# A recurrent layer's input projection: weights and input split into high and low parts, three products in place of one

## The reference, cut to what matters

```python
hn = rmsnorm(h, pre_mix_g[i])
proj = hn @ rwkv_w_in[j]                       # 1024 x 2816, float32
prev = jnp.pad(proj, ((0, 0), (1, 0), (0, 0)))[:, :-1]
xs = proj + (prev - proj) * mu                 # shift by one token
r, k, v, wl, al, gl = jnp.split(xs, offs, axis=-1)
w = -jax.nn.softplus(-(w0 + jnp.tanh(wl) @ w2)) - 0.5
a = jax.nn.sigmoid(a0 + al @ a2)
g = jax.nn.sigmoid(gl) @ g2
kk = kk * lax.rsqrt(jnp.maximum(jnp.sum(kk * kk, axis=-1, keepdims=True), 1e-24))
```

## Time and profile before

| What | Value |
| --- | --- |
| median of three runs | 764.7 us (764.57 to 766.06) |
| the profiled execution | 763.77 us, span in the trace 762.0 us |
| TensorE busy | 720.8 us, 95% of the span |
| VectorE, ScalarE, GpSimd busy | 444.2, 393.3, 106.8 us |
| recurrent strips in the span | 363.9 to 456.6 us |
| chunk phase begins | 463.56 us |

### The profile page before, as it was taken

One profiled execution on the slowest core, in us unless ns is written; L12 is line 12 of the kernel. 1 busy time (PEld: TensorE's weight loads), 2 busy tenths in 40 slices (PEclk: granted clock), 3 DMA queues, 4 the chain that ended last, 5 costly groups with the idle time before them and its releaser, 6 DMA issues.

```text
span 762.0 us, 15191 instructions
## 1 busy us (share of the span) xinstructions
PE 720.8 (95%) x6549; PEld 619.1 (81%) x6549; DVE 444.2 (58%) x645; ACT 393.3 (52%) x655; POOL 106.8 (14%) x163
## 2 busy tenths in 40 slices
PE   4999998999999999999999998987799999999997
PEld 3789975678888888888888878986678888888885
DVE  3778777646865675532243548642657757656523
ACT  5744776547655555532465536533258554556311
POOL 8121066700000000000300055700000000000000
PEclk9999989999999999999999999999999999999999
DMA  8846710007665565653844331000028565655511
GB/s 301 320 143 198 272 56 2 2 0 256 215 201 186 183 204 171 211 172 113 270 136 156 111 111 58 4 6 4 3 84 276 180 206 168 206 180 185 203 55 56
DMA packets 78277, 111.71 MB, mean 147 GB/s; under 512 B 2124, under 2 KB 64738, under 8 KB 78210
## 3 DMA queue, kind: packets, MB, share of 16 engines
q1 hardware_dynamic: 77090, 107.67, 42.3%
q0 software_dynamic: 976, 3.04, 1.3%
q10 hardware_dynamic: 144, 0.04, 0.0%
HBM read 109.68 MB, written 1.05 MB: 145 GB/s over the span
## 4 chain that ended last, share of the span: by engine, by line
PE 87%; DVE 5%; ACT 4%; issue 2%; DMA 1%; POOL 0%; DVEq 0%; SPq 0%; ACTq 0%; POOLq 0%
PE ps L1060 20%; PE ps L746 10%; PE ps L747 10%; PE ps L748 10%; PE ps L1063 10%; PE ps L1048 8%; PE ps L1225 5%; PE ps L1235 4%; PE ps L780 2%; PE ps L866 2%; PE ps L889 2%; DVE w_lo L1889 2%; PE ps L915 1%; DMA hn<-mem 1%; ACT w_hi L1416 1%
## 5 line engine op out<-in xcount | busy, mean ns | idle before, releaser
L1889 DVE TENSOR_TENSOR w_lo<-w_raw,w_hi 128x2048 fp32r<-128x2048 f32 (+2 forms) x90 | 202.2, 2260 | 84.4 <-ACT w_hi L1416 84.3
L1060 PE MATMUL ps<-x_hi_lo,w_hi 128*128 128x512 f32 x640 | 201.2, 396 | 0.0
L1416 ACT ACTIVATE w_hi<-w_raw 128x2048 fp32r<-128x2048 f32 (+2 forms) x90 | 168.1, 1887 | 39.4 <-PE ps L748 38.2
L1063 PEld LDWEIGHTS ps<-x_hi_lo,w_lo 128*128 128x128 f32 x640 | 120.2, 188 | 28.4
L1063 PE MATMUL ps<-x_hi_lo,w_lo 128*128 128x256 f32 x640 | 125.7, 278 | 0.0
L1060 PEld LDWEIGHTS ps<-x_hi_lo,w_hi 128*128 128x128 f32 x640 | 97.4, 189 | 0.0
L746 PE MATMUL ps<-w_hi,x_hi_lo 128*128 128x512 f32 (+3 forms) x208 | 74.0, 356 | 5.2 <-DVE x_hi_lo L2117 3.4
L748 PE MATMUL ps<-w_hi,x_hi_lo 128*128 128x512 f32 (+3 forms) x208 | 72.0, 346 | 0.0
L747 PE MATMUL ps<-w_lo,x_hi_lo 128*128 128x512 f32 (+3 forms) x208 | 71.9, 346 | 0.0
L746 PE MATMUL ps<-w_hi,hidden_hi 128*128 128x512 f32 x176 | 68.6, 390 | 0.0
L747 PE MATMUL ps<-w_lo,hidden_hi 128*128 128x512 f32 x176 | 68.5, 389 | 0.0
(11 more groups left out here) (367 smaller groups left out, 984.7 us busy)
## 6 DMA issues: line engine op xcount, KB each, us to landing
w_raw<-w_ffn_in SPq DMA_DIRECT2D x44, 1024.0 KB, 5.1
w_raw<-w_ffn_out SPq DMA_DIRECT2D x22, 1024.0 KB, 4.9
w_raw<-rwkv_w_in SPq DMA_DIRECT2D x11, 1024.0 KB, 5.1
w_raw<-w_out SPq DMA_DIRECT2D x8, 1024.0 KB, 5.0
w_raw<-nsa_w_in SPq DMA_DIRECT2D x6, 1024.0 KB, 14.5
w_raw<-w_mem_kv SPq DMA_DIRECT2D x2, 1024.0 KB, 9.4
w_raw<-nsa_cmp_k_w SPq DMA_DIRECT2D x2, 1024.0 KB, 5.7
w_raw<-nsa_cmp_v_w SPq DMA_DIRECT2D x2, 1024.0 KB, 5.4
```

The lines of the kernel that those rows point to most:

```text
L1060: pe.matmul(psum[:, bank + j, :], kt_of(w_hi, i, k)[:, cols[j]], xx[:, k, :, :].rearrange("p c n -> p (c n)"), start=k == 0, stop=False)
L1063: ins = pe.matmul(psum[:, bank + j, 0:SEQ], kt_of(w_lo, i, k)[:, cols[j]], xh[:, k, :], start=False, stop=k == KD - 1)
L1416: act.activation(w_hi[:, i % SPL, 0:size(i)], raw[:, i % RAW, 0:size(i)], ACT.Copy).then_inc(hi_done, 1)
L1889: dve.tensor_tensor(w_lo[:, i % RAW, 0:size(i)], raw[:, i % RAW, 0:size(i)], w_hi[:, i % SPL, 0:size(i)], ALU.subtract).then_inc(lo_done, 1)
```

## The change

`whole` and all that hung on it is removed. Pieces of the recurrent projection go through the same copy on ScalarE and subtraction on VectorE as all others; join 1 writes `x_hi_lo` in place of `x_rwkv`, as the other joins do; and both kinds of strip form each product by `three`. The positions of the `split_to` calls are not touched, but those that did nothing now split. The semaphore counts follow. Cut to its core:

```diff
         def tile_base(m, t):
-            return (0, 8, 12)[m] + (2 if m == 1 else 4) * t
+            return 4 * (TT * m + t)
@@ tok_strip
-                if whole(i):
-                    pe.wait_ge(landed[i % RAW], land_value[i])
-                else:
-                    pe.wait_ge(lo_done, split_no(i) + 1)
+                pe.wait_ge(lo_done, i + 1)
                 for k in range(KD):
-                    if whole(i):
-                        if part == 0 and k % 2 == 0:
-                            pe.wait_ge((j_hi, j_lo)[k // 2 % 2], tile_base(m, t) + k // 4 + 1)
-                        ins = pe.matmul(psum[:, turn_bank(m, t) + part, 0:FC], xf[:, k, tile(t)], raw_kt(i, k),
-                                        start=k == 0, stop=k == KD - 1)
-                        continue
@@ feature_strip
-                pe.wait_ge(landed[i % RAW], land_value[i])
+                pe.wait_ge(lo_done, i + 1)
                 for j in range(2):
                     c = slice(P * j, P * j + P)
                     for k in range(KD):
-                        ins = pe.matmul(psum[:, bank, j * SEQ:(j + 1) * SEQ], raw_kt(i, k)[:, c], xf[:, k, :],
-                                        start=k == 0, stop=k == KD - 1)
+                        ins = three(psum[:, bank, j * SEQ:(j + 1) * SEQ], kt_of(w_hi, i, k)[:, c], kt_of(w_lo, i, k)[:, c],
+                                    xh[:, k, :], xl[:, k, :], start=k == 0, stop=k == KD - 1)
@@ tile_hi (tile_lo: the same for the other four slices)
-                    if m == 1:
-                        if k // 2 % 2 == 0:
-                            ins = act.activation(xf[:, k, tile(t)], quarter(m, t, k), ACT.Copy, scale=colA[:, col:col + 1])
-                            if k % 2:
-                                ins.then_inc(j_hi, 1)
-                        continue
```

More of the change, by code:

```diff
@@ L170, in trunk @@
         xh, xl = xx[:, :, 0, :], xx[:, :, 1, :]
-        xf = at(o_x, "x_rwkv", [P, KD, SEQ])
         o_hn = base[0]
@@ L1023, in full_gemm @@
                     if t == 0:
-                        pe.wait_ge(lo_done, split_no(i0 + j) + 1)
+                        pe.wait_ge(lo_done, i0 + j + 1)
                         if j < n_ready:
@@ L1885, in split_to @@
                 for i in range(split[0], min(n, NPIECES)):
-                    if whole(i):
-                        continue
-                    dve.wait_ge(hi_done, split_no(i) + 1)
+                    dve.wait_ge(hi_done, i + 1)
                     dve.tensor_tensor(w_lo[:, i % RAW, 0:size(i)], raw[:, i % RAW, 0:size(i)], w_hi[:, i % SPL, 0:size(i)],
@@ L2106, in tile_lo @@
                     col = NORM_COL[m + 2] + k
[L2107 to L2114, removed]
                     if k % 2 == 0:
```

## The result

The changed kernel took 770.16 us, the median of 10 runs (767.84 to 775.23); the kernel before, on the same chip, 765.57 us (10 runs, 764.52 to 766.83). The ratio is 1.0054, its 95% interval 1.0039 to 1.0070: slower by half a per cent. The forecast was 769.0 us against a median of 764.7, so +4.3 us; measured +4.6.

A forecast was written before the change was run, and what follows sets the result against it. TensorE owned 87% of the chain, but ScalarE's and VectorE's written order was to decide: +4.9 - 0.6 = +4.3 us at the chunk phase turns 763.77 into 768.1; with 0.93 to the median, 769.0 us (767.8 to 770.6).

The forecast's parts named there:

- (g): Split 10 delays the receptances' last shift: first row maximum 6.5 us later, TensorE waits about 4 us inside strip 9.
- (a): Behind the first feed-forward layer: pieces 0 and 1 are split in ScalarE's 17.06 us of idle, at no cost.
- (b): At the join: eight high parts on ScalarE, eight low on VectorE; two token strips save 2.3 us and pay 0.65.
- (c): Join's end: splits 2, 3, 4 precede the `strip_tok` copies; TensorE waits 1.3 us, leaving 0.35 of 1.65 us gained.
- (d): Strip 2 saves 1.15 us: second lora group starts at 387.35 instead of 388.83, but `vT` ends at 406.5 as before.
- (e): Splits 7, 8 on ScalarE and low parts 8, 9 on VectorE delay the `kk_squares`: end at 420.95, before 418.53.
- (f): ScalarE's logarithm comes at 421.0, strip 6's copy ends at 429.5; TensorE stands still 6.2 us ahead of strip 8.
- (h): VectorE catches up where it formerly waited: second probabilities' turn 4.9 us later, chunk products at 467.9 instead of 463.56.
- Spare time enough: Rival: splits land in idle moments of ScalarE and VectorE, 9.6 us saved, 755 us; chance 0.08.
- Slow steps: Rival: strip products' three steps are no faster than now, 0.144 us each, giving 772 us; chance 0.03.
- Cancel: Rival: low parts 8 and 9 finish before the head sums, logarithm at 418.5 as before, 763.5 to 766 us; chance 0.13.
- The clock: Rival: TensorE's holes halve its clock; strips 8, 9 cost 0 to 0.4 us, strip 10 1.2 to 2.4; 770 to 773; chance 0.2.

The follow-up runs named there:

- the filled hole: The changed kernel with 14 full-precision matmuls of constants put into TensorE's wait ahead of strip 8; 772.8 us, ratio 1.0093 to the kernel before.
- reordered: The changed kernel with all splits kept, their copies on ScalarE and subtractions on VectorE moved to later places; 761.48 and 760.65 us, ratios 0.9920 and 0.9881.
- the join's order alone: The changed kernel with only the join moved: ScalarE writes the first tile's token-shift strip ahead of splits 3 and 4, third copy still behind; 770.8 us, ratio 1.0044.
- the stretched run of the kernel before: The unchanged kernel before, profiled again with the same instructions; TensorE's were stretched and its one run took 2518.07 us.

## Why the prediction was right, step by step

The forecast's case held, and its price came out right for the reason it gave, but for two places where one thing made up for another: the clock in (g) and in strip 10. Times in after lie 0.77 us later from the join on (369.34 for 368.57); with that taken off:

- **(a)** `hn` came 0.77 us later than before; the changed kernel's other profile has it at 368.07, 0.5 us earlier than before. No cost is seen here.
- **(b), (c)** TensorE waits 1.04 us for the token strip (forecast 1.3) and starts its turn at 378.5 (379.05). This step was 0.5 us too dark. It does count: the forecast took its 0.35 us of gain on to the lora products in (d), and the chain of after runs over it.
- **(d)** `vT` ends at 406.3 (406.5). The second lora group starts at 387.0 (387.35).
- **(e)** The squares end at 420.65 (420.95), and this is the step that makes the loss: with two low parts moved behind them it is gone (1.0004).
- **(f)** The hole is 6.28 us (6.2), strip 8 starts at 429.4 (429.5), released by the copy named.
- **(g)** The first row maximum comes 6.1 us later (6.5). The wait for the exponentials was forecast at 4 us and is 1.31. It is not smaller by a mistake in the order: strip 8 ran its first half at half clock, 5.2 us from 430.20 to 435.42 where half a strip takes 2.9, and ate 2.3 us of it. With the clock held up by the filled hole the same wait is 3.66, with two subtractions moved 3.49.
- **(h)** The turn of the second probabilities is 4.35 us later (4.9), the chunk start 3.76 (4.3). This is the term that was oversized, by half a microsecond, 0.4 of it brought along from (g).

**The sum** gave +4.3 us, varied +3.1 to +5.9. The strips measured +3.76, the medians +4.6 (3.0 to 5.4 by the interval of the ratio).

**The rivals.** *Spare time enough* is wrong for this order, but largely true for another: of the 9.6 us that it names, reordering saves 6.5 and 7.6 in its two comparisons (768.03 to 761.48, 768.29 to 760.65). The idle shares of the busy table were real, and only the places of the splits kept them from being used. *Slow steps* is refuted: the rows above show 0.12 us. *Cancel* needed the squares on time, which two moved subtractions give, and their ratio of 1.0004 is that of a cancelled gain. Its sum was off: 2.5 and up to 1.2 us less than the forecast are 765.3 to 766.5, not 763.5 to 766, and the squares on time are worth 4.8 us at the row maximum, not 2.5.

*The clock* fell just where that rival said. The windows of after (length, then busy PE, PEld, DVE, ACT, POOL; granted clock, DMA share, GB/s):

```profile
424.00:428.00 4.00, 0.00 (x0) 0.00 (x0) 0.00 (x0) 3.99 (x4) 0.00 (x0) 1.00 0.71 241
428.00:432.00 4.00, 1.80 (x8) 1.83 (x9) 0.23 (x1) 4.00 (x7) 0.00 (x0) 0.54 0.06 26
432.00:436.00 4.00, 4.00 (x22) 3.58 (x20) 4.00 (x3) 0.23 (x1) 0.00 (x0) 0.61 0.00 0
436.00:440.00 4.00, 4.00 (x32) 3.49 (x31) 3.93 (x8) 0.00 (x0) 0.00 (x0) 1.00 0.02 4
...
448.00:452.00 4.00, 1.29 (x10) 0.89 (x11) 3.28 (x5) 0.71 (x3) 3.82 (x3) 1.00 0.71 233
452.00:456.00 4.00, 4.00 (x23) 4.00 (x22) 1.53 (x4) 2.44 (x9) 1.77 (x3) 0.57 0.09 29
```

After 6.28 us of standing still the clock is 0.54, near the level of 1.2 GHz, and the steps of strip 8 start 0.21 us apart (430.98, 431.19 above). It is back at 1.00 from 436 on. The Trainium skill, "TensorE: Matmul & The Clock Gate", Part 1, has this as its rule: idle halves the clock, sustained work restores it. The trace agrees. The lowered clock cost nothing in the strips: both slow stretches of after lie where TensorE waits behind them anyway, strip 8 for the exponentials and strip 10's first half for ScalarE's first copy of the probabilities, which ends at 456.25 + 0.59 = 456.84, just ahead of the turn at 456.94. The median of 770.16 also lies in this rival's 770 to 773, but its mechanism, slow strips that reach the end, did not happen.

For strips 8 and 9 that is the reason the forecast gave. For strip 10 it had a price, 1.2 to 2.4 us, and left it out only because its row was of mixed small work: there it was right by luck. How much can hang on it is shown by reordered, whose two profiles are of one program. In the first, strip 10's first half is the slow one, and from its probabilities to the next turn it takes 446.70 to 450.25, 3.55 us; in the second, the second half is slow and takes 445.81 to 450.89, 5.08 us, and the strips 1.5 us more. The rival's 1.2 to 2.4 us for strip 10 is thus the right price, to be paid where the stretch falls uncovered. In both profiles of the changed kernel, and in that of the join's order alone, it fell covered, so there it may be more than chance.

**What stays open.** Whether the changed kernel loses more in the chunk phase than the kernel before; what an order without the wait for the token strip would bring; why the slow stretch of strip 10 falls now on one half and now on the other, and the stretched run of the kernel before.

## What to carry to other kernels

When work is added to engines with idle time, look at the instructions in front of which it stands, not at the idle share: moving two subtractions, 4.5 us, from ahead of the squares to behind them turned +0.5% into nothing, and placing all splits by that rule turned it into -0.8 and -1.2%. Place such work right behind the operation that others wait for, as late as its own reader allows. In a written order, walk ahead of time the chain of every engine that frees a buffer for the fast one; the walk gave the hole to 0.1 us before the kernel ran.

## What the runs showed of the hardware

- In after a hole of 6.28 us, and one of 2.71 us, were both followed by some 5 us at half clock (windows at 0.54 to 0.61, and at 0.57): a rounded 256-column step then takes 0.21 us in place of 0.12. A hole of 1.87 us was followed by such a stretch in one profile of reordered (0.66) and not in the other (1.00).
- Filling one hole with dummy products did not remove such stretches here, it moved them: with the first hole filled, the next wait grew from 1.31 to 3.66 us and was followed by a window at 0.60.
- One program can gain or lose 1.5 us in one place by where such a stretch falls (reordered, two profiles), and 2.4 us in the chunk phase (before, 82.45 and 84.84). A single profile's span is uncertain by that much, while the stretch from join to `rT` agrees to 0.01 us where the clock does not differ.
